# Where the last square of a norm is added: TensorE's accumulation or GpSimd's running sum

## The reference

```python
def rmsnorm(x, g):
    xf = x.astype(jnp.float32)
    y = xf * lax.rsqrt(jnp.mean(xf * xf, axis=-1, keepdims=True) + EPS)
    return (y * g.astype(jnp.float32)).astype(x.dtype)

def modulate(x, g, shift, scale):
    return rmsnorm(x, g) * (1.0 + scale) + shift
```

## Time and profile before

| | us |
|---|---|
| median of 3 runs | 996.98 |
| lowest and highest run | 996.24, 997.82 |
| the profiled execution | 997.2 |
| its span, first to last instruction | 995.4 |
| TensorE busy | 949.8 (95%) |
| VectorE, ScalarE, GpSimd busy | 714.8, 539.2, 300.9 |
| mean granted TensorE clock | 0.975 of full speed |
| adds of squares on GpSimd (L2126) | 36, on `square_sum` 30 of them with 1293 ns in the mean |

### The profile page before, as it was taken

How to read it: one execution, slowest core, us unless ns; L and a number is a source line. 1 busy time by engine, 2 the same in 40 slices (tenths; PEclk the granted TensorE clock), 3 DMA queues, 4 the chain that set the end, 5 groups by cost and what they waited for, 6 DMA issues and landing times.

```text
span 995.4 us, 19561 instructions
## 1 busy us (share of the span) xinstructions
PE 949.8 (95%) x6898; PEld 874.0 (88%) x6898; DVE 714.8 (72%) x1131; ACT 539.2 (54%) x920; POOL 300.9 (30%) x256
## 2 busy tenths in 40 slices
PE   5998989999999999999979999999999999999996
PEld 5877556799999999988969999999999768899996
DVE  3997778678888777897986787555555873475774
ACT  3465555465765444654635566654444761674555
POOL 1942002227897011120051288641110000320012
PEclk9898999999999999999979999999999998999998
DMA  9856145167978877788615686555655332255521
GB/s 340 295 181 240 46 178 167 32 233 272 321 273 268 292 267 282 248 316 287 222 59 185 217 275 211 176 184 176 192 190 173 106 107 85 85 170 173 167 86 43
DMA packets 55773, 194.56 MB, mean 195 GB/s; under 512 B 6047, under 2 KB 8511, under 8 KB 55456
## 3 DMA queue, kind: packets, MB, share of 16 engines
q1 hardware_dynamic: 55312, 192.36, 56.9%
q0 software_dynamic: 400, 1.39, 0.5%
HBM read 192.65 MB, written 1.07 MB: 195 GB/s over the span
## 4 chain that ended last, share of the span: by engine, by line
PE 83%; DVE 11%; issue 3%; ACT 2%; DMA 1%; POOL 0%; SPq 0%; DVEq 0%; ACTq 0%
PE bank L522 24%; PE bank L523 23%; PE bank L524 23%; DVE w_lo L1568 2%; PE bank L784 1%; PE bank L620 1%; PE bank L775 1%; DMA x<-x_in 1%; PE bank L944 1%; PE bank L918 1%; PE bank L817 1%; PE bank L629 1%; PE bank L872 1%; ACT w_hi L1139 1%; DVE ada_raw L1670 1%
## 5 line engine op out<-in xcount | busy, mean ns | idle before, releaser
L1568 DVE TENSOR_TENSOR w_lo<-raw,w_hi 128x1024 fp32r<-128x1024 f32 (+1 forms) x261 | 340.0, 1304 | 107.3 <-ACT w_hi L1139 104.5
L1139 ACT ACTIVATE w_hi<-raw 128x1024 fp32r<-128x1024 f32 (+1 forms) x261 | 272.4, 1044 | 173.2 <-PE bank L524 165.2
L522 PE MATMUL bank<-act_hi,w_hi 128*128 128x258 f32 (+1 forms) x872 | 251.5, 288 | 0.0
L523 PE MATMUL bank<-act_lo,w_hi 128*128 128x258 f32 (+1 forms) x872 | 248.2, 285 | 0.0
L524 PE MATMUL bank<-act_hi,w_lo 128*128 128x258 f32 (+1 forms) x872 | 247.7, 284 | 0.0
L522 PEld LDWEIGHTS bank<-act_hi,w_hi 128*128 128x128 f32 x872 | 166.2, 191 | 3.2 <-issue 2.8
L523 PEld LDWEIGHTS bank<-act_lo,w_hi 128*128 128x128 f32 x872 | 166.1, 190 | 1.0 <-issue 1.0
L524 PEld LDWEIGHTS bank<-act_hi,w_lo 128*128 128x128 f32 x872 | 166.1, 191 | 0.0
L523 PE MATMUL bank<-hid_lo,w_hi 128*128 128x256 f32 x512 | 143.9, 281 | 0.0
L524 PE MATMUL bank<-hid_hi,w_lo 128*128 128x256 f32 x512 | 143.4, 280 | 0.0
L522 PE MATMUL bank<-hid_hi,w_hi 128*128 128x256 f32 x512 | 142.3, 278 | 0.0
(11 more groups left out here) (347 smaller groups left out, 1823.8 us busy)
## 6 DMA issues: line engine op xcount, KB each, us to landing
raw<-weights SPq DMA_DIRECT2D x247, 512.0 KB, 3.9
ada_raw<-ada SPq DMA_DIRECT2D x88, 512.0 KB, 4.9
raw<-weights SPq DMA_DIRECT2D x14, 384.0 KB, 4.2
ada_more<-ada SPq DMA_DIRECT2D x8, 512.0 KB, 6.4
bias<-bias_by_distance SPq DMA_DIRECT2D x1, 2048.0 KB, 9.3
x<-x_in SPq DMA_DIRECT2D x1, 1024.0 KB, 8.2
ctx<-ctx_in SPq DMA_DIRECT2D x1, 1024.0 KB, 10.2
out<-result SPq DMA_DIRECT2D x4, 256.0 KB, 2.7
```

The costliest lines, as they stand in the source:

```text
L522: pe.matmul(dst, w[0], a[0], start=start, stop=False)
L523: pe.matmul(dst, w[0], a[1], start=False, stop=False)
L1139: act.activation(w_hi[:, slot, 0:width_of(c)], raw[:, slot, 0:width_of(c)], ACT.Copy).then_inc(weight_hi, 1)
L1568: dve.tensor_tensor(w_lo[:, slot, 0:w], raw[:, slot, 0:w], w_hi[:, slot, 0:w].bitcast(fp32), ALU.subtract).then_inc(weight_lo, 1)
```

## The change

In the first five norms GpSimd makes seven adds in place of six, so that `square_sum` holds all eight squares. TensorE waits for the seventh and makes one product in place of two; by token, one product of one column for each half of the tokens in place of two. In the sixth norm nothing is computed otherwise: GpSimd makes six adds there, and the counts that are waited for follow the new numbering of `square_sums`.

```diff
             def sum_squares(norm, by_token=False):
 
-                pe.wait_ge(square_sums, norm * (KT - 2))
-                pe.matmul(bank[4][:, 0:S], mean[:], square_sum[:], start=True, stop=False)
-                pe.wait_ge(squared, squares_before(norm) + KT)
-                last = pe.matmul(bank[4][:, 0:S], mean[:], sq[:, KT - 1, :], start=False, stop=True)
+                pe.wait_ge(square_sums, norm * (KT - 1))
+                last = pe.matmul(bank[4][:, 0:S], mean[:], square_sum[:], start=True, stop=True)
                 if by_token:
                     for tt in range(2):
-                        for part in (square_sum[:, tt * P:(tt + 1) * P], sq[:, KT - 1, tt * P:(tt + 1) * P]):
-                            last = pe.matmul(bank[4][:, S + tt:S + tt + 1], part, mean[:, 0:1],
-                                             start=part.tensor is square_sum, stop=part.tensor is not square_sum)
+                        last = pe.matmul(bank[4][:, S + tt:S + tt + 1], square_sum[:, tt * P:(tt + 1) * P],
+                                         mean[:, 0:1], start=True, stop=True)
                 last.then_inc(sums_ready, 1)
...
-            pe.wait_ge(square_sums, 6 * (KT - 2))
+            pe.wait_ge(square_sums, 5 * (KT - 1) + KT - 2)
...
             def sum_squares(norm):
 
-                for k in range(1, KT - 1):
+                for k in range(1, KT - 1 if norm == 6 else KT):
                     pool.wait_ge(squared, squares_before(norm) + k + 1)
                     if k > 1:
-                        pool.wait_ge(square_sums, (norm - 1) * (KT - 2) + k - 1)
+                        pool.wait_ge(square_sums, (norm - 1) * (KT - 1) + k - 1)
                     pool.tensor_tensor(square_sum[:], sq[:, 0, :] if k == 1 else square_sum[:], sq[:, k, :],
                                        ALU.add).then_inc(square_sums, 1)
```

## The result

| | before, us | changed, us | ratio, 95% interval |
|---|---|---|---|
| first measurement, 8 runs each | 997.07 (996.24 to 999.46) | 1004.33 (1002.5 to 1007.88) | 1.0073 (1.0061 to 1.0084) |
| a second chip, 9 runs of the change | 997.78 | 1002.62 (999.69 to 1005.76) | 1.0045 (1.0026 to 1.0064) |
| a third chip, 10 runs of the change | 997.41 | 1002.82 (999.56 to 1007.02) | 1.0060 (1.0041 to 1.0080) |

The change costs 7.3 us in the first measurement, 4.8 and 5.4 us in the two later ones. The forecast was 4.8 us. The first median lies 0.1 us above the range given, the other two inside it. The changed kernel also spreads more: its runs cover 5 to 8 us, those of before 3 to 5.

A forecast was written before the change was run, and what follows sets the result against it. TensorE, busy 95% of the span with 83% of the chain, was taken as the bound; 7.84 us of waits less 3.03 us of removed products gave 4.81 us slower, 1002.0 us profiled or 1001.8 us from the median, range 999.8 to 1004.2 us.

The forecast's parts named there:

- The place and sign: At the product of the sums in five norms: TensorE would wait for GpSimd's add, making the kernel 4.81 us slower.
- The removed work: On TensorE in five norms: one product each, 2.15 us, and one-column products in two norms, 0.88 us; together 3.03 us.
- The new add: On GpSimd in each norm: it ends 1.23 plus 0.59 us after the start of VectorE's conversion of weights.
- rule of exclusion: At the new add: read to the letter, the whole 0.74 us add follows VectorE's conversion; 1002.5 us, 6 in 100.
- the lower bound of the prediction: At the new add: it runs alone at 0.74 us, each wait 0.73 us shorter; 998.1 us, 5 in 100.
- The waits by norm: On TensorE: waits of 7.84 us less removed products of 3.03 us, given as a net cost for each norm; 4.81 us.
- the rival on TensorE's clock: In one of the new gaps TensorE's clock falls, costing 2.4 to 4.8 us; 1004.2 to 1006.6 us, 8 in 100.
- the prediction's own sign of being wrong: In the profile after: the forecast is wrong if the granted clock shows 0.50 right behind a norm.
- Nothing was absorbed: Rival at the later waits for VectorE (6.2 us at the gated MLP): they absorb the first four norms' shift; 997.4 us, 6 in 100.

The follow-up runs named there:

- the longer gap: The changed kernel with the seventh add issued as four adds of 64 columns each: 1008.46 us against 997.41, ratio 1.0106.
- the two filled: The changed kernel with matmuls that nobody reads ahead of TensorE's wait in the five norms, measured twice: 1001.42 us against 997.73, and 1002.04 against 997.41.
- the gain alone: The kernel before without the products that the change removes and with no seventh add: 994.19 us against 997.73, ratio 0.9962.
- the two with the square first: ScalarE's square of a finished tile moved ahead of its conversion of weights: in the changed kernel 995.69 us, in the kernel before 997.06 us, against 997.78.
- the two with the product later: The changed kernel with the product behind the second projection group: all five norms, 999.65 us; norms 1 to 4 with the square moved ahead, 994.67 us.

## Why the prediction was right in its sum and short in its total

**The place and sign** were right: five waits of TensorE on GpSimd's add, where none stood before.

**The removed work**, 3.03 us: the products taken out alone gave 3.5 us, with the interval from 2.2 to 5.4, and 3.2 us at full clock.

**The new add**, from the conversion's start plus 1.23 plus 0.59 us: it measured 1.22 or 1.23 plus 0.58 or 0.59. The Trainium skill's rule of exclusion ("SBUF — State Buffer", section "SBUF: two separate sides"), read to the letter, would have put the end 0.15 us later; the trace agrees with the exclusion and not with that. With the conversion out of the way the add took 0.74 us, the lower bound of the prediction.

**The waits by norm**: 0.91, 1.35, 1.28, 0.85 and 0.42 us were forecast, and 0.86 to 0.88, 1.35, 1.27 to 1.31, 0.81 to 0.87 and 0.34 to 0.51 are in the traces where the clock didn't fall.

**The step that failed** is the rival on TensorE's clock. I made it all or nothing, a long fall of 2.4 to 4.8 us with 8 chances in 100, and left it out of the likeliest case, and the prediction's own sign of being wrong, a granted clock of 0.50 right behind a norm, came true. It is a term of the sum: a fall of 3.4 us, worth 1.5 to 1.6 us, behind some of the norms. In the four profiles with gaps of 1.0 to 1.5 us it came behind 5 of 20 norms, with the longer gap behind 3 of 5, and in the eight profiles without a gap or with one under 0.2 us (before, the two filled, the gain alone, the two with the square first, the two with the product later) behind none of 40. Five of 20 would be 1.25 a run, 1.9 us. The clocks of all 27 runs of the changed kernel give less, 1.1 us in the mean: 2.2 us in the first measurement and 0.3 and 1.1 in the later ones, for falls elsewhere come and go as well. With the 4.6 us at full clock that is the measured 7.3, 4.8 and 5.4 us, within 0.5 us. That the first median passed the end of the range by 0.1 us, and the two others didn't, is chance.

The argument that let me set it aside was one stretch of the earlier trace rows where a gap of 1.41 us left the clock alone. That row was true and proved too little: three gaps in four leave it alone. The trace of the kernel before had the rest. TensorE waits there for 1.0 to 1.9 us at nine places that lie away from its long falls, and behind two of them the clock fell for 3.4 us, at 61.8 and 130.1 us, 0.8 and 1.2 us after the wait's end:

```profile
60.97 0.36 PE L522 MATMUL bank<-mla_in_hi,w_hi 128*128 128x256 f32 x1 [1.91 <-POOL mla_in_lo L2146]
...
62.00:63.00 1.00, 1.00 (x5) 0.90 (x5) 1.00 (x2) 1.00 (x2) 0.00 (x0) 0.50 0.09 37
...
128.93 0.49 PE L739 MATMUL bank<-k_rstd_hi,heads 8*128 8x512 f32 x1 [1.32 <-DVE k_rstd_lo L1788]
...
131.00:132.00 1.00, 1.00 (x4) 0.76 (x3) 0.22 (x1) 0.00 (x0) 0.00 (x0) 0.50 1.04 426
```

Two in nine, five new gaps and 1.5 us each would have put 1.7 us into the sum, from rows that were there.

**Nothing was absorbed** in total: at full clock the whole cost is there in all three measurements. The wait at the gated MLP is 6.2 us in both first profiles and 5.7 and 5.6 us in the two later ones of the changed kernel, but it is as short in kernels where nothing comes later.

**Open:** what decides behind which gap the clock falls. The filled kernel's interval of norm 2 is 0.65 us shorter than the sum says; the wait at the gated MLP in it is 5.6 us for 6.2, and in the kernel before with its square moved, where no norm costs anything, both are shorter by the same 0.7 us. With the square first in the changed kernel the two don't match, so this is a likeness and no proof, and why that wait differs stays open too.

## What to carry to other kernels

An operation moved from the busiest engine to an idle one is free only if its input is there early. Here the last input was ready within 0.4 us of its use, so look for the last arrival, not for the share of busy time, and move the producer ahead first: the same edit behind a reordered square gained about 2 us in place of losing 5 to 7. In this kernel a new gap on TensorE of a microsecond or more cost its own length and, in the mean, a part of a clock fall on top. Price it as a chance times 1.5 us in each place, not as one rare case, and take the chance from all the gaps of that length that the trace before already has, not from one.

## What the runs showed of the hardware

GpSimd's add of two 128x256 tiles ended 0.58 to 0.61 us after the end of a VectorE operation with two SBUF inputs that had begun before it, whether that was a conversion of 1.23 us or the remainder of 0.49 us, and took 0.74 us alone. That is as if about 0.15 us of the add ran under the other operation.

The granted clock fell to 0.50 behind 8 of 25 gaps of 1.0 to 1.9 us at the norms, and behind 2 of 9 such gaps elsewhere in the kernel before, 0.4 to 2.6 us after the gap's end, while TensorE ran the float32 products behind the norm or the matmuls after them, and came back after 3.4 us. With the gap filled by matmuls it fell behind none of 10. Longer falls elsewhere in the kernel were 6.8 or 10.2 us long, and differed between executions of one kernel.
